# Two-layer hybrid trunk on one core: when VectorE's search of experts yields to lowering, how it merges, and when the first activations are loaded

## The reference

```python
q = (h @ wq).reshape(B, T, 8, 2, 128)
s = einsum('bthpd,pnd->bthpn', q, subkeys)          # 128 scores per head and side
s_top, i_top = top_k(s, 16)
cand = s_top[..., 0, :, None] + s_top[..., 1, None, :]   # 16 x 16 sums
best, pos = top_k(cand.reshape(..., 256), 16)
experts = the key pair i_top[0] * 128 + i_top[1] of each pick
gates = softmax(best)
a = einsum('td,tkd->tk', hx, u[e])                  # 8 x 16 picks per token
y = einsum('tk,tkd->td', gates * gelu(a), v[e])
```

## Time and profile before

| | us |
|---|---|
| Timed runs, median of 3 | 3818.95 |
| lowest and highest | 3815.77, 3824.24 |
| The profiled execution's own time | 3855.64 |
| its span, first to last instruction | 3853.8 |
| TensorE's matmuls busy in it | 3758.7 |
| its mean granted TensorE clock | 0.991 |

### The profile page before, as it was taken

One profiled execution on the slowest core, in us unless ns is written; L12 is line 12 of the kernel. 1 busy time (PEld: TensorE's weight loads), 2 busy tenths in 40 slices (PEclk: granted clock), 3 DMA queues, 4 the chain that ended last, 5 costly groups with the idle time before them and its releaser, 6 DMA issues.

```text
span 3853.8 us, 47176 instructions
## 1 busy us (share of the span) xinstructions
PE 3758.7 (98%) x17288; PEld 3044.7 (79%) x17288; DVE 2394.1 (62%) x3962; ACT 1435.7 (37%) x2059; POOL 2049.0 (53%) x1486
## 2 busy tenths in 40 slices
PE   7999999999999999999999999999999999999999
PEld 5767878788878878888877678787877888788887
DVE  5736558977812237888766363489677222488887
ACT  4537533333323333333345373323323333333332
POOL 2432333477766537777434223335777666476772
PEclk9999999999999999999999999999999999999999
DMA  7656463576665459999847554436766754899995
GB/s 291 221 186 209 163 240 106 202 255 226 225 228 197 147 207 377 373 389 370 295 155 247 177 193 143 156 113 238 241 230 208 245 173 135 284 376 380 370 364 209
DMA packets 395414, 919.33 MB, mean 239 GB/s; under 512 B 64352, under 2 KB 136928, under 8 KB 395136
## 3 DMA queue, kind: packets, MB, share of 16 engines
q1 hardware_dynamic: 288384, 715.37, 53.6%
q0 software_dynamic: 69632, 134.82, 9.9%
q10 hardware_dynamic: 37248, 67.33, 4.7%
HBM read 844.33 MB, written 257.56 MB: 286 GB/s over the span
## 4 chain that ended last, share of the span: by engine, by line
PE 85%; DVE 8%; DMA 2%; issue 2%; ACT 1%; POOL 1%; another core or an unknown queue 0%; SPq 0%; ACTq 0%; DVEq 0%; POOLq 0%
PE ps L1074 16%; PE ps L1076 16%; PE ps L1075 16%; PE ps L1092 9%; PE ps L1093 9%; PE ps L1094 9%; DMA g_in<-expert_gate 1%; PE ps L1349 1%; PE ps L1353 1%; PE ps L1351 1%; PE ps L1316 1%; PE ps L1330 1%; DMA raw<-in_stream_dram 1%; POOL acts L1015 1%; PE ps L1306 1%
## 5 line engine op out<-in xcount | busy, mean ns | idle before, releaser
L1026 POOL DMA_INDIRECT expert_gate<-gate_v,gate_i x768 | 865.2, 1127 | 413.1 <-issue 197.2
L1010 POOL TENSOR_TENSOR w_lo<-raw,w_hi 128x1024 fp32r<-128x1024 f32 x178 | 443.5, 2492 | 906.9 <-ACT w_hi L620 906.9
L1074 PE MATMUL ps<-h_hi,w_hi 128*128 128x512 f32 x1776 | 702.5, 396 | 20.9 <-ACT gel L944 8.7
L1075 PE MATMUL ps<-h_hi,w_lo 128*128 128x512 f32 x1776 | 695.2, 391 | 0.0
L1076 PE MATMUL ps<-h_lo,w_hi 128*128 128x512 f32 x1776 | 694.9, 391 | 0.0
L620 ACT ACTIVATE w_hi<-raw 128x1024 fp32r<-128x1024 f32 x380 | 401.1, 1056 | 747.8 <-PE ps L1076 440.9
L944 ACT ACTIVATE gel<-ps 128x512 f32<-128x512 f32 x256 | 153.1, 598 | 828.5 <-PE ps L1076 546.1
L1015 POOL DMA_INDIRECT acts<-expert_act,e_act x256 | 352.7, 1378 | 170.9 <-DMA expert_act<-gel 93.5
L1035 POOL DMA_INDIRECT down<-expert_down,e_row x256 | 329.9, 1289 | 212.4 <-DVE y L1962 87.8
L1074 PEld LDWEIGHTS ps<-h_hi,w_hi 128*128 128x128 f32 x1776 | 334.5, 188 | 101.9 <-issue 26.6
L1074 PE MATMUL ps<-h_hi,w_hi_up 128*128 128x512 f32 x992 | 390.6, 394 | 16.4 <-issue 14.9
(11 more groups left out here) (291 smaller groups left out, 6949.2 us busy)
## 6 DMA issues: line engine op xcount, KB each, us to landing
raw<-in_stream_dram SPq DMA_DIRECT2D x648, 512.0 KB
expert_down<-in_stream_dram SPq DMA_DIRECT2D x256, 512.0 KB
expert_act<-gel ACTq DMA_DIRECT2D x256, 256.0 KB
raw_more<-in_stream_dram SPq DMA_DIRECT2D x128, 512.0 KB
expert_gate<-zeros SPq DMA_DIRECT2D x96, 512.0 KB, 6.1
a_in<-expert_act SPq DMA_DIRECT2D x128, 384.0 KB
g_in<-expert_gate SPq DMA_DIRECT2D x128, 384.0 KB
expert_gate<-gate_v,gate_i POOLq DMA_INDIRECT x768
```

Of the source, the lines that this page charges most:

```text
L1010: pool.tensor_tensor(w_lo[:, s, :], raw[:, b, :], w_hi[:, s, :].bitcast(F32), ALU.subtract).then_inc(lo_ready, 1)
L1026: pool.indirect_dma_start(out=gate_d[l], out_offset=bass.IndirectOffsetOnAxis(ap=gate_i[:, tt, h, c:c + 1], axis=0), in_=gate_v[:, tt, h, ...
L1074: pe.matmul(o, sta_hi[:, w], mov_hi[:, c, :], start=c == 0, stop=False)
L1075: pe.matmul(o, sta_lo[:, w], mov_hi[:, c, :], start=False, stop=False)
```

## The change

It does four things. (1) `lower_next` is no longer called after each phase; each phase reports a number of elements, `pace` adds them up, and at every 3700 (`STRIDE`) one unit is lowered. The counts: a phase of `top16` on four tiles of 256 reports 1536, or 3072 where it does two operations; the sums of `experts_of` report 2048; a side of `choose` 3000, 2500 and 2200; a pass of `merge` on one tile 256h + 100. In group 0 three units are lowered, after `choose`, `weigh` and the merges. (2) `merge` goes tile by tile, nine smaller passes in place of three. (3) The loads of the first four activation pairs (`a_in`) are issued right after the raw load of unit 121, with the waits that they need; only the gates' loads (`g_in`) stay behind the wait for the puts. (4) `EXP_AT` and `PUT_UNITS` get new values.

```diff
-EXP_AT = (7, 20, 37, 55)
+EXP_AT = (7, 18, 31, 46)
...
-PUT_FIRST, PUT_UNITS = 9, 112
+PUT_FIRST, PUT_UNITS = 9, 110
+STRIDE = 3700
...
+                def load_acts(pair, b):
+                    sp.dma_start(a_in[:, b], act_units[bass.ds(pair * 2, 2), :, P:SEQ].rearrange("i j t -> j i t")
+                                 ).then_inc(ag_loaded[b], 16)
+
                 for m in range(U_WQ + 2 * RAW, U_U + 124):
                     load_split(l, m, m % RAW)
                     if 0 <= m - U_U < NK - COPIES_M:
                         copy_down(l, COPIES_M + m - U_U)
+                    if m == U_U + 121:
+                        sp.wait_ge(picked_ready, (l + 1) * PH)
+                        for s in range(2):
+                            sp.wait_ge(gel_stored[s], 16 * (l * (NK // 2) + 12) + 16)
+                        for b in range(4):
+                            load_acts(b, b)
...
                 for tt in range(DT):
                     sp.wait_ge(gate_put[tt], (l + 1) * PICKS * 16)
-                for s in range(2):
-                    sp.wait_ge(gel_stored[s], 16 * (l * (NK // 2) + 12) + 16)
                 for b in range(4):
-                    load_pair(b, b)
+                    load_gates(b, b)
...
+                def pace(elements):
+
+                    nonlocal passed
+                    passed += elements
+                    if passed >= STRIDE:
+                        passed -= STRIDE
+                        lower_next()
...
-                    both = [P, DT, TOPK, n]
-                    hit = same[:, :DT * TOPK * n].rearrange("p (t k m) -> p t k m", t=DT, k=TOPK)
...
-                    step(tt_op(hit, mine, earlier, ALU.is_equal))
-                    between()
-                    step(tt_op(hit, hit, weights, ALU.mult))
-                    between()
-                    step(dve.tensor_reduce(own, hit, AX_X, ALU.add))
-                    between()
+                    both = [P, TOPK, n]
+                    for tt in range(DT):
+                        hit = same[:, tt * TOPK * n:(tt + 1) * TOPK * n].rearrange("p (k m) -> p k m", k=TOPK)
...
+                        step(tt_op(hit, mine, earlier, ALU.is_equal))
+                        between(TOPK * n + 100)
+                        step(tt_op(hit, hit, weights, ALU.mult))
+                        between(TOPK * n + 100)
+                        step(dve.tensor_reduce(own[:, tt], hit, AX_X, ALU.add))
+                        between(TOPK * n + 100)
...
                 for g in range(4):
-                    pace = lower_next if g else lambda: None
-                    experts_of(2 * g, pace)
-                    experts_of(2 * g + 1, pace)
-                    choose(g, pace)
+                    paced = pace if g else no_pace
+                    experts_of(2 * g, paced)
+                    experts_of(2 * g + 1, paced)
+                    choose(g, paced)
+                    if g == 0:
+                        lower_next()
                     weigh(g)
-                    merge(2 * g, pace)
-                    merge(2 * g + 1, pace)
+                    if g == 0:
+                        lower_next()
+                    merge(2 * g, paced)
+                    merge(2 * g + 1, paced)
+                    if g == 0:
+                        lower_next()
```

More of the change, by code:

```diff
@@ L573, in _, with load_gates @@
                         copy_down(l, COPIES_M + m - U_U)
+                    if m == U_U + 121:
[4 more added lines that the diff above has]
+                            load_acts(b, b)
                 def load_pair(pair, b):
+                    load_acts(pair, b)
+                    load_gates(pair, b)
+                def load_gates(pair, b):
                     src = bass.ds(pair * 2, 2)
-                    sp.dma_start(a_in[:, b], act_units[src, :, P:SEQ].rearrange("i j t -> j i t")
-                                 ).then_inc(ag_loaded[b], 16)
                     sp.dma_start(g_in[:, b], gate_units[l][src].rearrange("i j t -> j i t")).then_inc(ag_loaded[b], 16)
@@ L1787, in _ @@
                 tt_op(sub_lo[:], sub_raw[:], sub_hi[:].bitcast(F32), ALU.subtract).then_inc(sub_ready, 1)
-                lowered = LOW0
+                lowered, passed = LOW0, 0
                 def lower_next():
@@ L1799, in lower_next, with no_pace, top16 @@
                         lowered += 1
-                def top16(vals, rest_v, tops, idx, count, between=lambda: None):
+                def pace(elements):
[4 more added lines that the diff above has]
+                        lower_next()
+                def no_pace(elements):
+                    pass
+                def top16(vals, rest_v, tops, idx, count, between=no_pace):
+                    width = vals(0).shape[-1] * 3 // 2
                     for j in range(count):
@@ L1805, in top16 @@
                     settle(ins)
-                    between()
+                    between(count * width)
                     for j in range(count):
@@ L1814, in top16 @@
                     settle(ins)
-                    between()
+                    between(2 * count * width)
                     for j in range(count):
@@ L1840, in _, with experts_of @@
                     sub_keys(n)
-                def experts_of(h, between=lambda: None):
+                def experts_of(h, between=no_pace):
                     for tt in range(TT):
@@ L1848, in experts_of @@
                     settle(ins)
+                    between(TT * 512)
                     top16(lambda j: cand[:, j, :], lambda j: rest[:, j, :], lambda j: best[:, j, h, :],
@@ L1855, in tiles_of, with choose @@
                     return a.rearrange("p (t k) -> p t k", t=TT)
-                def choose(g, between=lambda: None):
+                def choose(g, between):
                     hs = slice(2 * g, 2 * g + 2)
@@ L1871, in choose @@
                         step(tt_op(match[:], iota16, half_f[:].unsqueeze(2).to_broadcast([P, PICKS, TOPK]), ALU.is_equal))
-                        between()
+                        between(3000)
                         for hh in range(2):
@@ L1877, in choose @@
                         step(ins)
+                        between(2500)
                         step(dve.tensor_reduce(picked[:, side, :], match[:], AX_X, ALU.add))
-                        between()
+                        between(2200)
                     ids = e_id[:].rearrange("p t k -> p (t k)")
@@ L1900, in weigh, with merge @@
                     step(tt_op(gate_r[:, :, hs, :], best[:, 1:TT, hs, :], share[:, 1:TT], ALU.mult))
-                def merge(h, between=lambda: None):
+                def merge(h, between):
                     own, n = gate_v[:, :, h, :], h * TOPK
@@ L1907, in merge @@
                         return
-                    both = [P, DT, TOPK, n]
-                    hit = same[:, :DT * TOPK * n].rearrange("p (t k m) -> p t k m", t=DT, k=TOPK)
-                    mine = gate_f[:, :, h, :].unsqueeze(3).to_broadcast(both)
-                    earlier = gate_f[:, :, 0:h, :].rearrange("p t h k -> p t (h k)").unsqueeze(2).to_broadcast(both)
-                    weights = gate_r[:, :, 0:h, :].rearrange("p t h k -> p t (h k)").unsqueeze(2).to_broadcast(both)
-                    step(tt_op(hit, mine, earlier, ALU.is_equal))
-                    between()
-                    step(tt_op(hit, hit, weights, ALU.mult))
-                    between()
-                    step(dve.tensor_reduce(own, hit, AX_X, ALU.add))
-                    between()
+                    both = [P, TOPK, n]
+                    for tt in range(DT):
+                        hit = same[:, tt * TOPK * n:(tt + 1) * TOPK * n].rearrange("p (k m) -> p k m", k=TOPK)
+                        mine = gate_f[:, tt, h, :].unsqueeze(2).to_broadcast(both)
+                        earlier = gate_f[:, tt, 0:h, :].rearrange("p h k -> p (h k)").unsqueeze(1).to_broadcast(both)
+                        weights = gate_r[:, tt, 0:h, :].rearrange("p h k -> p (h k)").unsqueeze(1).to_broadcast(both)
+                        step(tt_op(hit, mine, earlier, ALU.is_equal))
[4 more added lines that the diff above has]
+                        between(TOPK * n + 100)
                     tt_op(own, own, gate_r[:, :, h, :], ALU.add).then_inc(picked_ready, 1)
```

## The result

| | us |
|---|---|
| Kernel before, median of 4 | 3817.36 (3813.48 to 3824.24) |
| Changed kernel, median of 4 | 3791.78 (3790.79 to 3792.28) |
| Ratio, 95% interval | 0.9931 (0.9914 to 0.9948) |
| Profiled execution, before | 3855.64 |
| Profiled execution, changed | 3792.22, span 3790.4 |

The timed runs gain 25.6 us, the two profiled executions 63.4. A reader who compared the two profiles alone would have believed the second number.

What follows compares the result with a forecast made beforehand. TensorE was taken as the bound, its matmuls busy 98% of the span. Early lowering -12.0 and handover -13.0, with pacing, merges and exponentials 0, gave -25 us: 3794 us, own range 3784 to 3803, overall 3764 to 3811.

Steps and rivals of the forecast that it cites:

- A: TensorE's stop at expert unit 12, lost 5.7 and 6.3 us; early lowering was to remove it, -12.0 us.
- D: TensorE's loss near unit 122, 7.5 and 5.4 us, from a late raw load; handover was to save 13.0 us.
- The others have more room: Group 0 lowerings of units 13 and 14 have more time to spare than unit 12's 3.2 us.
- unit 125's load comes 17.8 us sooner where 13.2 were missing: Handover step: earlier gates 10.9, fewer issues 2.4 and half the remaining time 4.5 us bring the raw load forward.
- with the gates alone 2 us stay missing: Handover bound: earlier puts without moved activation loads would leave unit 125's raw load 2 us late.
- Rival 3: TensorE still waits once a layer at some later unit; only gates' 10.9 us help: 3813 us, chance 0.08.
- 95.1 us is all that a reordering of the other engines can reach: From the page: TensorE's matmuls are busy 98% of the span, so only its stops could be recovered.
- B and C: Losses near units 45 and 65 in each layer, together 34.3 us, taken as mostly absent from timed runs.
- rival 1: Losses near units 45 and 65 are real, from crowding transfers, and pacing removes them: 3760 us, chance 0.20.
- Rival 4: Lowering lags in the search because a count is not a time, so TensorE waits at every unit: 3834 us, chance 0.06.
- nearly as much again: Clock cost at 1.2 GHz after stalls, added to 11.5 us a layer lost if lowering lags at 5.9 us steps.
- 2: Only unit 12's stop goes; the late load near unit 122 remains or moves: 3807 us, chance 0.14.

Runs made afterwards that it cites:

- the second comparison: The changed kernel, unaltered, timed again beside the kernel before and three part-edits: 3793.61 us, ratio 0.9934.
- e3_both: Kernel before plus three lowerings in group 0 and the new handover, without pacing by elements, split merges or new exponential units: 3792.39 us, ratio 0.9929.
- e5: Changed kernel without the three group 0 lowerings and with the old handover: 3825.07 us, ratio 1.0016.
- e2: Kernel before with only the new handover, PUT_UNITS 110 and four activation loads moved ahead: 3808.59 us, ratio 0.9970.
- e9: Kernel before, unchanged, run once more for a second profile: median 3818.75 us, profiled execution 3817.74 us.

## Why the prediction was right, and where not

The forecast was -25 us; the runs gave -25.6 and, in the second comparison, -26.5. The sum came closer than its terms: A gave up to 2.3 us more than forecast and D 1.5 less, both inside the intervals.

**The first lowering (A).** -12.0 forecast; 14.3 and 12.7 measured with three and with one. The reason given holds: the lowering starts at 755.21, its upper half long ready, and ends before TensorE comes. "The others have more room" was true to the point that they did not need to be moved.

**The handover (D).** -13.0 forecast, 11.5 measured; the direction and size hold, a step of it failed. It was "unit 125's load comes 17.8 us sooner where 13.2 were missing", and its bound "with the gates alone 2 us stay missing". The 13.16 us were ScalarE's idle time before a split that TensorE needs only later. What TensorE missed was its own stop, 4.6 us, so 4 to 5 us of earliness were needed and not 13. The 17.8 was too much as well: ScalarE's wait shrank by 10.0 us with the puts and 4.9 with the activations, 14.9 together. Rival 3, in which D "half stays" with the gates alone, rested on the same mistake.

**What can be reached.** "95.1 us is all that a reordering of the other engines can reach" was a wrong reading of the earlier trace rows. TensorE's busy time includes matmuls at the lower clock and is not fixed: it fell by 21.8 us for the same matmuls. The sum did not use the 95.1, but matmul counts, which have the clock's part in them.

**The timed runs against the profile (B and C).** That these 34.3 us were mostly absent from timed runs was right, and it decided the forecast: taking them as real gave 3760 (rival 1). Two things show it: A's and D's edits alone carry the whole gain, and a second profile of the same kernel has no B and C. The reason offered beside it, that they belong to the profiler, is not shown. Recording alone does not cost it: 13 further profiled executions of twelve kernels lie between 4.4 us below and 3.2 us above their kernels' medians, among them the changed kernel's 3792.22, which is itself one of its four timed runs. By the rule that the Trainium skill states (NOTIFIC — the notification-queue block, 7.1), an engine can be held back by full queues; no run here shows whether that happened in the first profile. What is seen is that this profile's records are incomplete: its trace holds 33,828 semaphore increments where the other 13 hold 52,964 to 53,138, and of the semaphore by which TensorE reports finished units 623 where they hold 696 to 698. Near B and C the next recorded increment of that semaphore stands up to 7.8 and 14.4 us behind the end of a unit's matmuls; in the second profile it stands 0.01 to 0.02 us behind. With increments unrecorded, a releaser may be named "remote" or "issue", so that name, on which the prediction leaned, is weak evidence in this profile. So the recording was disturbed together with the kernel; which disturbed which is not shown. The cause stays open. The difference between the two profiles, 63.4 us, is no measure of the change.

**Pacing by elements.** 0 us forecast, 0 measured (e3_both against the changed kernel, 3792.39 and 3793.61). The price of 1.06 us per 1000 counts was good: at 4500 and 5400, where VectorE sets the pace, the steps were 6.06 and 6.93 us, which less 1.22 are 1.08 and 1.06 per 1000. At 3700 the steps were 5.27 us (unit 15 at 768.9, unit 61 at 1011.5) and not 5.1, since VectorE there waits at times for the upper half. Rival 4's threshold, a mean step of 5.65 us, lies between 5.27, which loses nothing, and 6.06, which loses 17.5 us a layer; it was worked out with 10 us in hand, and with the 6.3 to 6.5 that the runs show it would be 5.57. Its second term, the slow clock that costs "nearly as much again", was wrong: in both runs VectorE's lag is the whole price.

**Merges by tile.** +7.5 us of VectorE a layer forecast, 15.2 in two measured on the page. Covered, as said. That the cover matters shows in e5, where the one merge in front of the first lowering cost 1.1 us a layer.

**Rivals.** 1, 2 and 3 fell with e2, e3 and e9; 4 needs a stride of over 3700. What the new profile was to show came in: no `w_lo` wait, gates' wait 12.5 us, the raw wait gone, 3.5 to 7.4 us between lowerings after the first two, never three in a row, the search over at 1009.6 us (1002 to 1017 forecast), as TensorE came to unit 58, with unit 60 the last lowered.

## What to carry to other kernels

Where one profiled execution is 1% over the timed median, sort the stops by cause before summing: those with a late producer in the program recurred here in a second profile, those with a release late for no reason did not, and a second profile costs one run. Idle time of a feeding engine is not the amount by which its input is late for the bottleneck; subtract the slack, here 8.6 of 13 us. The uncovered work stood here at the two ends of the expert stretch: one early lowering and a two-step shift in a constant did what a new pacing scheme was written around.

## What was not expected of the hardware

The clock's part of a stop depends on what sets the pace. In the second profile of the kernel before, TensorE waited 4.28 us at unit 12, and the 10 us around it hold 19 matmuls: 5.7 us lost, 1.4 more than the wait, at a granted clock of 0.83.

```profile
762.95 0.79 PE L1074 MATMUL ps<-h_hi,w_hi 128*128 128x512 f32 x1 [4.28 <-DVE w_lo L1797]
```

That excess is paid in full: the waits at unit 12 add up to 8.5 us in both layers, and taking them away gave 12.7 to 14.3. With STRIDE 4500 twelve waits of the first layer add up to 10.5 us and 17.5 are lost, 0.6 more for each than its recorded wait, yet the loss is no more than VectorE's lag of 24.0 less the 6.5 in hand.

The other thing is the first profile itself: a disturbance of 34 us, in both layers near the same units, that none of 13 later profiled executions repeated.
